# Expert stage: the loop's head on an instruction block, gate/up in two turns on TensorE, a fourth weight buffer, low parts one step later

## The chip, the cores and the metric

One core of a Trainium2 chip runs the whole program. The metric is the device time of one execution in microseconds, the median of the runs. The engines are TensorE (PE), VectorE (DVE), ScalarE (ACT), GpSimd (POOL) and SyncE (SP), which here issues the DMAs of the weights. Each engine has a sequencer of its own that runs that engine's instructions, loops and branches; engines meet at semaphores.

## The reference

One layer of an encoder over 2048 tokens of width 1024. First token mixing: a combined projection, banded attention in 8 heads, differential attention in 4 heads, an output projection. Then channel mixing, in which the change lies: each token goes to 4 of 32 experts.

```
logits = hf @ w_router + b_router;  top_v, top_i = top_k(logits, 4);  top_w = softmax(top_v)
gu   = ragged_dot(xs, w_gate_up, group_sizes) + b_gate_up      # 1024 -> 2 x 1024, per expert
gate = minimum(gu[:, :1024], 7);  up = clip(gu[:, 1024:], -7, 7)
act  = (up + 1) * (gate * sigmoid(1.702 * gate))
y    = ragged_dot(act, w_down, group_sizes) + b_down           # 1024 -> 1024, per expert
out  = segment_sum(y * top_w, token)
```

All of it is in float32.

## The kernel before

Stages 1 and 2 compute the modulation, the normalised input and the attention; stage 3 the output projection, the router and the lists of tokens per expert; stage 4 the experts; stage 5 the final norm. Only stage 4 (`stage4`) is touched. Routing gives every expert its list, and the list is cut into tiles of 320 tokens (`TOK`), the rest going into one tile of 256 (`SMALL`) where it fits. `table` holds the counts. The inputs of this case give 33 tiles, 15 of 320 and 18 of 256.

TensorE, ScalarE and VectorE each run `over_sizes`: a loop over the 32 experts that loads four numbers of the table (the number of large tiles, whether there is a small one, and two from `expert_tiles`), then, under an If, a loop over the large tiles, then, under an If, the small tile. So the code of a tile stands twice in each engine's loop, once for each size. SP and POOL have a loop of their own, `over_tiles`.

A float32 product is made of three products of a shorter format: each operand is split into a high and a low part, and high x high, high x low and low x high are summed in PSUM. A tile's weights are 12 units of 128 x 2048 numbers: 8 units of gate/up (one for each of the 8 blocks of 128 hidden columns, `m`), then 4 of the down projection (`d`). Two units are a pair. SP loads pairs into 3 raw slots (`load_pair`), each when the low parts of the pair that had the slot are made (`lo_ok`). ScalarE makes the high part `hi` (`split_hi`, L1306), VectorE the low part `lo` = raw - hi (`split_lo`, L1347), each into one of `SPL` = 3 buffers. Both are called for the unit `SPL` ahead of the one that TensorE has just used (`split_next`).

Gate/up step `m` on TensorE (L1265 to L1267): 2 outputs x 8 blocks x 3 = 48 matmuls into two of four PSUM banks, after waits for the low part of the unit and, from `m` = 2, for the eviction of step `m` - 2 (`g_ev`). The 8 steps are written out. VectorE evicts gate and up with bias and clamp (L1382, L1386, L1389), makes the low part of the last step's activation (`a_lo`, L1361), then the weights' low part (L1347), waits for ScalarE's sigmoid (L1326), and multiplies (L1394, L1395). ScalarE makes the sigmoid, the weights' high part (L1306), then `a_hi` (L1329).

The down phase has 4 units, 2 column halves x 2 halves of the sum. A step `d` takes the tile's 128-token parts in turn (2 for 256 tokens, 3 for 320, the last of 64), 12 matmuls each (L1287 to L1290). Between them TensorE transposes the next tile's rows in six batches (L1252), which ScalarE and VectorE split into `x_hi` (L1319) and `x_lo` (L1356) from a single PSUM bank. After the odd steps VectorE adds the bias and scales by router weight and gate (`result`, L1369 and L1372). POOL scatters the result rows and adds them in HBM, then gathers the rows of the tile after the next.

Of the kernel before, what the change touches and what calls it, by code (L numbers as in the profile page):

```python
# [1101 lines left out]
def stage4(nc, io, sb, sem, bank, ident, mod_d, acc_d, h2_d, list_d, table):  # L1102
# [9 lines left out]
    RAW, SPL = 3, 3  # L1112
    UPT, PPT = 12, 6
    MT = D // P
    def subtiles(tok):
        return [(s, min(P, tok - s * P)) for s in range(-(-tok // P))]
# [7 lines left out]
    with ExitStack() as ctx:  # L1124
# [30 lines left out]
        LO0 = 2 * RAW  # L1155

# [6 lines left out]
        def over_sizes(eng, tile):  # L1163

            with eng.Fori(0, NE) as e:
                full = eng.value_load(table[0:1, bass.ds(e + 3 * NE, 1)], min_val=0, max_val=CAP // TOK)
                small = eng.value_load(table[0:1, bass.ds(e + 4 * NE, 1)], min_val=0, max_val=1)
                _, before = expert_tiles(eng, e)

                with eng.If(full > 0):  # L1170
                    with eng.Fori(0, full) as r:
                        tile(e, before + r, TOK)
                with eng.If(small > 0):
                    tile(e, before + full, SMALL)
# [31 lines left out]
        with nc.Block() as block:  # L1206
# [37 lines left out]
            def _(pe):  # L1244
# [10 lines left out]
                def tile(e, g, tok):  # L1255
                    pe.wait_ge(xlo_ok, NX * g + NX)
                    for m in range(MT):
                        pe.wait_ge(lo_ok, UPT * g + m + 1 + LO0)
                        if m >= 2:
                            pe.wait_ge(g_ev, 2 * MT * g + 2 * (m - 2) + 2)  # L1260
                        for o in range(2):
                            out = bank[2 * (m % 2) + o][:, 0:tok]
                            for k in range(KT):
                                at = slice((o * KT + k) * P, (o * KT + k + 1) * P)
                                pe.matmul(out, hi[m % SPL][:, at], x_hi[:, k, 0:tok], start=(k == 0), stop=False)  # L1265
                                pe.matmul(out, hi[m % SPL][:, at], x_lo[:, k, 0:tok], start=False, stop=False)  # L1266
                                mm = pe.matmul(out, lo[m % SPL][:, at], x_hi[:, k, 0:tok], start=False,  # L1267
                                               stop=(k == KT - 1))
                            mm.then_inc(gu_mm, 1)
# [32 lines left out]
            def _(act):  # L1302
# [20 lines left out]
                def tile(e, g, tok):  # L1323
                    for m in range(MT):
                        act.wait_ge(g_ev, 2 * MT * g + 2 * m + 1)
                        act.activation(sig[:, 0:tok], gate[:, 0:tok], ACT.Sigmoid, scale=ALPHA).then_inc(sig_ok, 1)  # L1326
                        split_next(m, g)
                        act.wait_ge(a_ok, MT * g + m + 1)
                        act.activation(a_hi[:, m, 0:tok], a[:, m % 2, 0:tok], ACT.Copy).then_inc(ahi_ok, 1)  # L1329
                    for d in range(4):  # L1330
# [12 lines left out]
            def _(dve):  # L1343
# [5 lines left out]
                def split_next(u, g):  # L1349
                    split_lo((u + SPL) % UPT, g + (u + SPL) // UPT)  # L1350
# [24 lines left out]
                def tile(e, g, tok):  # L1375
# [3 lines left out]
                    for m in range(MT):  # L1379
# [8 lines left out]
                        dve.wait_ge(g_ev, 2 * MT * g + 2 * m + 2)  # L1388
                        ch.link(dve.tensor_scalar(up[:, 0:tok], up[:, 0:tok], LIMIT, 1.0, ALU.min, ALU.add))  # L1389
                        if m:  # L1390
                            act_low(g, m - 1, tok)
                        split_next(m, g)
# [3 lines left out]
                        dve.wait_ge(a_ok, MT * g + m + 1)  # L1396
                    act_low(g, MT - 1, tok)
# [4 lines left out]
                    for d in range(4):  # L1402
                        for s, rows in subtiles(tok):
# [4 lines left out]
                        split_next(MT + d, g)  # L1408
                    assert ch.n == NG

                dve.sem_inc(lo_ok, LO0)
                dve.wait_ge(cin, 48)
# [4 lines left out]
                for u in range(SPL):  # L1417
                    split_lo(u, 0)
# [170 lines left out]
```

## Time and profile before

| | |
|---|---|
| median of 3 runs | 5525.59 us (5518.23 to 5529.43) |
| profiled execution, its time and its span | 5522.5 us |
| mean granted TensorE clock | 0.914 |
| TensorE matmul busy | 4660.9 us, 84% of the span |
| TensorE weight loads busy | 3782.0 us, 68% |
| VectorE busy | 3050.0 us, 55% |
| ScalarE busy | 1813.7 us, 33% |
| GpSimd busy | 538.1 us, 10% |
| DMA | 655.59 MB, mean 119 GB/s |

Busy shares are means over stages with different limits; the expert stage is a little over half of the span. A line such as `DVE w_lo L1347` names the engine, the tile written and the line. A "q" behind an engine's name means its sequencer.
### The profile page before, as it was taken

How to read it: one execution, taken by the hardware profiler on the slowest of the kernel's cores; microseconds unless marked ns; L12 is line 12 of the kernel's file. 1: busy time of each engine (PE TensorE's matmuls, PEld its weight loads, DVE VectorE, ACT ScalarE, POOL GpSimd, SP SyncE). 2: the span in 40 equal slices, each digit the busy share in tenths (PEclk: the TensorE clock that was granted, in tenths of full speed). 3: DMA queues.
4: the chain of work that ended last, by engine and by line, in shares of the span. 5: the costliest groups of instructions: out<-in, count | busy, mean ns of one | idle time of the engine just before them, and what ended most of it. 6: DMA issues, size and time to landing. Idle time of an engine off the chain costs nothing. (4 is left out here: it accounts for less than half of the span.)

```text
span 5522.5 us, 75366 instructions
## 1 busy us (share of the span) xinstructions
PE 4660.9 (84%) x25330; PEld 3782.0 (68%) x25331; DVE 3050.0 (55%) x5885; ACT 1813.7 (33%) x2483; POOL 538.1 (10%) x564
## 2 busy tenths in 40 slices
PE   6598987967778658849888999899999999998984
PEld 1565666744545534429787888888888888887873
DVE  3214444065665734436666756666666566666655
ACT  0123333132332312213333433333333333333434
POOL 1000000000000002121111010101010101011111
PEclk9799999988888878869999999999999999999997
DMA  6200001000000042235555555556454456555555
GB/s 228 76 9 20 13 20 32 0 14 11 7 13 3 7 156 76 76 113 174 168 189 173 188 156 183 176 165 191 161 173 165 148 185 199 175 169 184 189 160 204
DMA packets 461031, 655.59 MB, mean 119 GB/s; under 512 B 23036, under 2 KB 334980, under 8 KB 460568
## 3 DMA queue, kind: packets, MB, share of 16 engines
q1 hardware_dynamic: 419240, 523.11, 28.0%
q0 software_dynamic: 39152, 120.42, 8.3%
q10 hardware_dynamic: 2304, 8.39, 0.4%
q8 instruction: 113, 1.85, 0.1%
q14 instruction: 222, 1.82, 0.1%
HBM read 567.71 MB, written 87.27 MB: 119 GB/s over the span
## 5 line engine op out<-in xcount | busy, mean ns | idle before, releaser
L1265 PE MATMUL bank<-x_hi,w_hi 128*128 128x256 f32 (+1 forms) x4224 | 1273.0, 301 | 121.4 <-DVE up L1386 81.2
L1266 PE MATMUL bank<-x_lo,w_hi 128*128 128x256 f32 (+1 forms) x4224 | 1262.8, 299 | 0.0
L1267 PE MATMUL bank<-x_hi,w_lo 128*128 128x256 f32 (+1 forms) x4224 | 1262.0, 299 | 0.0
L1347 DVE TENSOR_TENSOR w_lo<-raw,w_hi 128x2048 fp32r<-128x2048 f32 x399 | 914.6, 2292 | 399.2 <-ACT w_hi L1306 396.5
L1265 PEld LDWEIGHTS bank<-x_hi,w_hi 128*128 128x128 f32 x4224 | 820.5, 194 | 145.2 <-DVE up L1386 90.8
L1306 ACT ACTIVATE w_hi<-raw 128x2048 fp32r<-128x2048 f32 x399 | 759.1, 1903 | 217.5 <-PE bank L1290 167.6
L1266 PEld LDWEIGHTS bank<-x_lo,w_hi 128*128 128x128 f32 x4224 | 821.2, 194 | 0.0
L1267 PEld LDWEIGHTS bank<-x_hi,w_lo 128*128 128x128 f32 x4224 | 819.9, 194 | 0.0
L1287 PE MATMUL bank<-w_hi,a_hi 128*128 128x512 f32 (+1 forms) x1296 | 540.2, 417 | 91.6 <-DVE a_lo L1361 91.6
L1289 PE MATMUL bank<-w_lo,a_hi 128*128 128x512 f32 (+1 forms) x1296 | 519.2, 401 | 0.0
L1290 PE MATMUL bank<-w_hi,a_lo 128*128 128x512 f32 (+1 forms) x1296 | 518.7, 400 | 0.0
L1436 POOL DMA_INDIRECT acc_scratch<-y,idc x102 | 214.8, 2106 | 2193.6 <-DVE y L1372 2172.7
L486 PE MATMUL bank<-v_all,PT 128*128 x2208 | 347.9, 299 | 93.0 <-DVE PT L504 50.5
L486 PEld LDWEIGHTS bank<-v_all,PT 128*128 128x128 f32 x2208 | 291.0, 201 | 152.9 <-issue 82.5
L1329 ACT ACTIVATE a_hi<-a 128x256 fp32r<-128x256 f32 (+1 forms) x264 | 116.8, 442 | 848.6 <-DVE a L1395 848.6
L608 PE MATMUL bank<-k_hi,q 128*128 128x512 f32 (+3 forms) x544 | 227.4, 423 | 171.3 <-DVE k_lo L701 89.9
L1287 PEld LDWEIGHTS bank<-w_hi,a_hi 128*128 128x128 f32 (+1 forms) x1296 | 239.3, 185 | 153.3 <-DVE a_lo L1361 95.9
L724 DVE CUSTOM_DVE_ANT_0 S<-bank,bias 128x512 f32<-128x512 f32 (+3 forms) x544 | 282.6, 559 | 35.4 <-PE bank L608 23.9
L1290 PEld LDWEIGHTS bank<-w_hi,a_lo 128*128 128x128 f32 (+1 forms) x1296 | 237.8, 183 | 70.9
L1289 PEld LDWEIGHTS bank<-w_lo,a_hi 128*128 128x128 f32 (+1 forms) x1296 | 239.7, 185 | 57.1
L646 ACT ACTIVATE S<-S,nm 128x640 f32<-128x640 f32 (+15 forms) x256 | 249.0, 975 | 73.1 <-DVE nm L735 44.3
L893 PE MATMUL bank<-wout,oT 128*128 128x512 f32 x512 | 260.3, 673 | 13.7 <-ACT oT L931 13.7
(211 smaller groups left out, 5695.5 us busy)
## 6 DMA issues: line engine op xcount, KB each, us to landing
raw<-in_w_gate_up SPq DMA_DIRECT2D x268, 1024.0 KB
raw<-in_w_down SPq DMA_DIRECT2D x132, 1024.0 KB
wada<-in_w_ada SPq DMA_DIRECT2D x12, 2048.0 KB, 7.9
bd<-in_b_down SPq DMA_DIRECT2D x33, 512.0 KB
xt<-in_x ACTq DMA_DIRECT2D x16, 512.0 KB, 6.0
o_scratch<-osb SPq DMA_DIRECT2D x128, 64.0 KB, 1.6
ot<-o_scratch SPq DMA_DIRECT2D x16, 512.0 KB, 3.3
xt<-in_x SPq DMA_DIRECT2D x16, 512.0 KB, 3.9
```

Of the source, the lines that this page charges most:

```text
L486: mm = pe.matmul(obank[t % 2][:, h * P:(h + 1) * P], PT[:, i % 4, j * P:(j + 1) * P], v_all[:, kt + j, bass.ds(u * P, P)], start=(first an ...
L646: act.activation(scores(step % 2, c)[:, 0:n], scores(step % 2, c)[:, 0:n], ACT.Exp, bias=nm[:, step % 2, c:c + 1], accum_out=l[:, step % 2 ...
L724: dve.tensor_tensor_reduce(scores(b, c)[:, cs:cs + n * P], sbank[i % 4][:, 0:n * P], add, SCALE, NEG * 8, ALU.add, ALU.max, pm[:, b, c, j: ...
L893: mm = pe.matmul(bank[2 + h][:, :], oT[:, b, k, :], wout[:, k, h * 512:(h + 1) * 512], start=(k == 0), stop=(k == KT - 1))
L1265: pe.matmul(out, hi[m % SPL][:, at], x_hi[:, k, 0:tok], start=(k == 0), stop=False)
L1266: pe.matmul(out, hi[m % SPL][:, at], x_lo[:, k, 0:tok], start=False, stop=False)
L1267: mm = pe.matmul(out, lo[m % SPL][:, at], x_hi[:, k, 0:tok], start=False, stop=(k == KT - 1))
L1287: pe.matmul(out, a_hi[:, k, tk], hi[u % SPL][:, at], start=(kh == 0 and i == 0), stop=False)
L1289: pe.matmul(out, a_hi[:, k, tk], lo[u % SPL][:, at], start=False, stop=False)
L1290: mm = pe.matmul(out, a_lo[:, k, tk], hi[u % SPL][:, at], start=False, stop=(kh == 1 and i == 3))
L1306: act.activation(h, src, ACT.Copy).then_inc(hi_ok, 1)
L1347: dve.tensor_tensor(l, src, h, ALU.subtract).then_inc(lo_ok, 1)
```

## The change

- `SPL` is 4: four buffers each for high and low parts.
- TensorE's gate/up is a loop of two turns of four steps each. The waits for evictions now stand ahead of every step; so that the first two pass, the semaphore `g_ev` starts at `G0` = 4, and all its other users add 4.
- VectorE makes the low part of unit m + 3 (`split_behind`), while ScalarE makes the high part of unit m + 4 in the same step. In gate/up it stands behind the multiplications and ahead of `a_lo`, which is now that of the same step; in the down phase it stands ahead of a step's results, not behind.
- ScalarE makes `a_hi` ahead of the weights' high part.
- `over_sizes` begins with an alignment: the code that follows is placed at the start of an instruction block of 256 on each of the three engines. One of its four table loads is left out, as its number isn't used.

```
--- before.py
+++ after.py
@@ -1109,7 +1109,7 @@
 
 
 
-    RAW, SPL = 3, 3
+    RAW, SPL = 3, 4
     UPT, PPT = 12, 6
     MT = D // P
     def subtiles(tok):
@@ -1153,6 +1153,7 @@
         raw_in = [sem(f"s4_raw_in{i}") for i in range(RAW)]
         NG = 2 * MT
         LO0 = 2 * RAW
+        G0 = 4
 
         def expert_tiles(eng, e):
 
@@ -1162,10 +1163,11 @@
 
         def over_sizes(eng, tile):
 
+            eng.addr_align(256, offset=0, max_nops=0)
             with eng.Fori(0, NE) as e:
                 full = eng.value_load(table[0:1, bass.ds(e + 3 * NE, 1)], min_val=0, max_val=CAP // TOK)
                 small = eng.value_load(table[0:1, bass.ds(e + 4 * NE, 1)], min_val=0, max_val=1)
-                _, before = expert_tiles(eng, e)
+                before = eng.value_load(table[0:1, bass.ds(e + NE, 1)], min_val=0, max_val=TOPK * SEQ // TOK + NE)
 
                 with eng.If(full > 0):
                     with eng.Fori(0, full) as r:
@@ -1253,20 +1255,20 @@
                     mm.then_inc(tx_mm, 1)
 
                 def tile(e, g, tok):
-                    pe.wait_ge(xlo_ok, NX * g + NX)
-                    for m in range(MT):
-                        pe.wait_ge(lo_ok, UPT * g + m + 1 + LO0)
-                        if m >= 2:
-                            pe.wait_ge(g_ev, 2 * MT * g + 2 * (m - 2) + 2)
-                        for o in range(2):
-                            out = bank[2 * (m % 2) + o][:, 0:tok]
-                            for k in range(KT):
-                                at = slice((o * KT + k) * P, (o * KT + k + 1) * P)
-                                pe.matmul(out, hi[m % SPL][:, at], x_hi[:, k, 0:tok], start=(k == 0), stop=False)
-                                pe.matmul(out, hi[m % SPL][:, at], x_lo[:, k, 0:tok], start=False, stop=False)
-                                mm = pe.matmul(out, lo[m % SPL][:, at], x_hi[:, k, 0:tok], start=False,
-                                               stop=(k == KT - 1))
-                            mm.then_inc(gu_mm, 1)
+                    with pe.Fori(0, MT // SPL) as q:
+                        pe.wait_ge(xlo_ok, NX * g + NX)
+                        for j in range(SPL):
+                            pe.wait_ge(lo_ok, UPT * g + SPL * q + j + 1 + LO0)
+                            pe.wait_ge(g_ev, 2 * MT * g + 2 * SPL * q + 2 * j - 2 + G0)
+                            for o in range(2):
+                                out = bank[2 * (j % 2) + o][:, 0:tok]
+                                for k in range(KT):
+                                    at = slice((o * KT + k) * P, (o * KT + k + 1) * P)
+                                    pe.matmul(out, hi[j][:, at], x_hi[:, k, 0:tok], start=(k == 0), stop=False)
+                                    pe.matmul(out, hi[j][:, at], x_lo[:, k, 0:tok], start=False, stop=False)
+                                    mm = pe.matmul(out, lo[j][:, at], x_hi[:, k, 0:tok], start=False,
+                                                   stop=(k == KT - 1))
+                                mm.then_inc(gu_mm, 1)
 
                     pe.wait_ge(xg_in, 16 * NS * g + 32 * NS)
                     for c in range(2):
@@ -1322,11 +1324,11 @@
 
                 def tile(e, g, tok):
                     for m in range(MT):
-                        act.wait_ge(g_ev, 2 * MT * g + 2 * m + 1)
+                        act.wait_ge(g_ev, 2 * MT * g + 2 * m + 1 + G0)
                         act.activation(sig[:, 0:tok], gate[:, 0:tok], ACT.Sigmoid, scale=ALPHA).then_inc(sig_ok, 1)
-                        split_next(m, g)
                         act.wait_ge(a_ok, MT * g + m + 1)
                         act.activation(a_hi[:, m, 0:tok], a[:, m % 2, 0:tok], ACT.Copy).then_inc(ahi_ok, 1)
+                        split_next(m, g)
                     for d in range(4):
                         for s in range(NS):
                             if (d, s) in batch_after[tok]:
@@ -1346,8 +1348,9 @@
                     src, h, l = split_views(u)
                     dve.tensor_tensor(l, src, h, ALU.subtract).then_inc(lo_ok, 1)
 
-                def split_next(u, g):
-                    split_lo((u + SPL) % UPT, g + (u + SPL) // UPT)
+                def split_behind(u, g):
+
+                    split_lo((u + SPL - 1) % UPT, g + (u + SPL - 1) // UPT)
 
                 def x_low(g, j):
                     (s, rows), h = subs[j // 2], j % 2
@@ -1385,36 +1388,36 @@
                         dve.wait_ge(gu_mm, 2 * MT * g + 2 * m + 2)
                         dve.tensor_scalar(up[:, 0:tok], bank[2 * (m % 2) + 1][:, 0:tok], bcur[:, MT + m:MT + m + 1], -LIMIT,
                                           ALU.add, ALU.max).then_inc(g_ev, 1)
-                        dve.wait_ge(g_ev, 2 * MT * g + 2 * m + 2)
+                        dve.wait_ge(g_ev, 2 * MT * g + 2 * m + 2 + G0)
                         ch.link(dve.tensor_scalar(up[:, 0:tok], up[:, 0:tok], LIMIT, 1.0, ALU.min, ALU.add))
-                        if m:
-                            act_low(g, m - 1, tok)
-                        split_next(m, g)
                         dve.wait_ge(sig_ok, MT * g + m + 1)
                         ch.link(dve.tensor_tensor(gate[:, 0:tok], gate[:, 0:tok], sig[:, 0:tok], ALU.mult))
                         dve.tensor_tensor(a[:, m % 2, 0:tok], up[:, 0:tok], gate[:, 0:tok], ALU.mult).then_inc(a_ok, 1)
-                        dve.wait_ge(a_ok, MT * g + m + 1)
-                    act_low(g, MT - 1, tok)
+                        if m < MT - 1:
+                            split_behind(m, g)
+                        act_low(g, m, tok)
+                    split_behind(MT - 1, g)
 
                     dve.wait_ge(bd_in, 16 * g + 16)
                     dve.wait_ge(idc_ok, NS * g + NS)
                     dve.wait_ge(sc, 16 * NS * g + 16 * NS)
                     for d in range(4):
+                        split_behind(MT + d, g)
                         for s, rows in subtiles(tok):
                             if d % 2 == 1:
                                 result(g, d // 2, s, rows, tok)
                             if (d, s) in batch_after[tok]:
                                 x_low(g + 1, batch_after[tok][d, s])
-                        split_next(MT + d, g)
                     assert ch.n == NG
 
                 dve.sem_inc(lo_ok, LO0)
+                dve.sem_inc(g_ev, G0)
                 dve.wait_ge(cin, 48)
 
                 dve.memset(xg[:, :, :], 0.0).then_inc(cleared, 1)
                 dve.wait_ge(cleared, 1)
                 dve.memset(y[:, :, :], 0.0).then_inc(go, 1)
-                for u in range(SPL):
+                for u in range(SPL - 1):
                     split_lo(u, 0)
                 for j in range(NX):
                     x_low(0, j)
```

## Rows read from the trace of the kernel before

**Rows 1.** Windows: start:end, length, busy us per engine (instructions), granted clock, DMA share, GB/s.

```profile
3008.20:3094.60 86.40, 75.29 (x504) 69.64 (x504) 55.50 (x77) 32.68 (x36) 11.70 (x12) 0.92 0.58 182
...
3094.60:3187.00 92.40, 92.19 (x552) 83.22 (x552) 61.10 (x80) 33.59 (x35) 11.48 (x12) 1.00 0.57 178
...
4576.50:4653.00 76.50, 71.25 (x505) 66.22 (x504) 58.39 (x78) 34.98 (x37) 16.55 (x13) 1.00 0.67 214
...
2491.20:5451.80 2960.60, 2751.16 (x17352) 2509.63 (x17352) 1917.20 (x2535) 1097.64 (x1154) 398.19 (x382) 0.96 0.55 174
```

**Rows 2.** Waits of 2480 to 5452 us: who, for whom, total us, times, longest.

```profile
DVE w_lo L1347 <- ACT w_hi L1306: 393.4, 393, 1.6
...
DVE bcur L1377 <- issue: 346.8, 32, 14.4
...
PE bank L1287 <- DVE a_lo L1361: 91.6, 18, 6.0
...
PE bank L1265 <- DVE up L1386: 81.2, 22, 7.9
...
ACT L1326 <- issue: 43.0, 32, 3.0
```

**Rows 3.** Timeline of VectorE and TensorE at a turn: start, us, instruction, idle before.

```profile
3024.32 0.17 DVE L1377 COPY bcur<-bgu 128x16 f32 x1 [12.11 <-issue]
...
3025.56 0.58 PE L1265 MATMUL bank<-x_hi,w_hi 128*128 128x256 f32 x1 [5.46 <-DVE up L1386]
```

**Rows 4.** Sequencer instructions of single lines: ns min/median/max, first and last start.

```profile
L1165 PEldq COMPARE_BRANCH  x32: 79/214/3548, 2564.9 to 5445.5; - x32
...
L1165 DVEq COMPARE_BRANCH  x1: 63/63/63, 3010.0 to 3010.0; - x1
L1165 DVEq FUSED_REGOPS  x1: 74/74/74, 3015.7 to 3015.7; - x1
...
L1170 DVEq COMPARE_BRANCH  x1: 56/56/56, 3020.5 to 3020.5; - x1
...
L687 DVEq FUSED_REGOPS  x1: 63/63/63, 490.4 to 490.4; - x1
```

**Rows 5.** Readers of `tile_table`: the load at the loop's head that the change leaves out.

```profile
L1159 DVEq TENSOR_LOAD <-tile_table x32: 298/432/991, 2487.4 to 5373.7; - x32
```

**Rows 6.** DMA queue of instructions, 3008 to 3026 us: packets, MB, share of the engines.

```profile
q14 instruction: 4, 0.03, 0.5%
```

**Rows 7.** Timeline of VectorE in gate/up: two low parts one step apart.

```profile
3039.37 2.29 DVE L1347 TENSOR_TENSOR w_lo<-raw,w_hi 128x2048 fp32r<-128x2048 f32 x1 [1.11 <-ACT w_hi L1306]
...
3045.36 2.29 DVE L1347 TENSOR_TENSOR w_lo<-raw,w_hi 128x2048 fp32r<-128x2048 f32 x1 [1.11 <-ACT w_hi L1306]
```

**Rows 8.** Timeline of TensorE in the small tile that starts at 4576.51.

```profile
4622.58 0.40 PE L1287 MATMUL bank<-w_hi,a_hi 128*128 128x512 f32 x1
...
4628.06 0.60 PE L1252 MATMUL bank<-ident,xg 128*128 128x128 f32 x4
4630.53 0.50 PE L1287 MATMUL bank<-w_hi,a_hi 128*128 128x512 f32 x1 [1.88 <-DVE a_lo L1361]
...
4653.01 0.38 PE L1265 MATMUL bank<-x_hi,w_hi 128*128 128x256 f32 x1 [3.37 <-issue]
```

**Rows 9.** Groups by line, 3008 to 3094 us; then the DMA queue, 3066 to 3073.

```profile
L1347 DVE TENSOR_TENSOR w_lo<-raw,w_hi 128x2048 fp32r<-128x2048 f32 x12 | 27.5, 2293 | 12.5 <-ACT w_hi L1306 12.5
...
L1306 ACT ACTIVATE w_hi<-raw 128x2048 fp32r<-128x2048 f32 x12 | 22.8, 1900 | 2.4 <-PE bank L1290 2.4
...
L1356 DVE TENSOR_TENSOR x_lo<-bank,x_hi 128x512 fp32r<-128x512 f32 (+1 forms) x6 | 3.6, 598 | 1.5 <-ACT x_hi L1319 1.5
...
L1372 DVE SCALAR_TENSOR_TENSOR y<-y,idc,gtf 128x512 f32<-128x512 f32 x4 | 3.0, 753 | 0.3
...
L1369 DVE TENSOR_TENSOR y<-bank,bd 128x512 f32<-128x512 f32 x4 | 2.8, 688 | 2.1 <-PE bank L1290 2.1
...
q1 hardware_dynamic: 2049, 2.07, 88.8%
```

## The prediction

> **What bounds the kernel now.** I read the windows first. The expert stage is 2960.6 us of the span [rows 1] and consists of 33 tiles, 18 of 256 tokens and 15 of 320. The reader is to compare three tiles there: a 320-token tile takes 92.4 us with TensorE busy 92.21, a 256-token tile in the middle takes 86.4 us with TensorE busy 75.29 at a granted clock of 0.92, and one 256-token tile, the second of its expert, takes 76.5 us at a clock of 1.00. So the large tiles are bound by TensorE, and the small ones lose some 10 to 20 us each.
>
> The waits say to what [rows 2]. TensorE waits 91.6 us, 18 times, ahead of the down projection for `a_lo`, 81.2 us ahead of a gate/up step for the eviction `up`. VectorE itself waits 346.8 us, 32 times, ahead of the first instruction of a tile (`bcur`) for nothing visible, and 393.4 us for ScalarE's `w_hi`. These two are the roots; POOL's and ScalarE's waits end ahead of nothing that TensorE waits for.
>
> Root one is the turn of the expert loop on VectorE. In [rows 3] `bcur` starts after 12.11 us idle. Its sequencer shows where they go [rows 4]: the branch back is taken at 3010.0 and the head goes on at 3015.7, 5.5 us later; the head (four table loads) lasts to 3020.5; the branch over the large body is taken there, and `bcur` behind it starts at 3024.3, 3.6 us of fetch later. The same turn costs ScalarE 43.0 us in 32 times, 1.3 us each, head and all [rows 2]. Instruction packets land in just these gaps: four of 8 KB between 3008 and 3026 [rows 6]. So the program's own code is being fetched. TensorE has it too, seldom: its branch back takes 79 ns to 3548 ns, median 214 [rows 4]; eight turns are slow (3.3 to 3.6), each at the end of a small tile that followed a large one.
>
> Root two is VectorE's step. Two `w_lo` in a row start 5.99 us apart, and 1.11 us of it is the wait for the `w_hi` that ScalarE makes in the same step [rows 7]. TensorE needs 384 matmuls x 0.120 us / 8 = 5.76 us a step of 256 tokens: 4576.51 to 4622.58 for eight [rows 8]. VectorE is thus slower than TensorE by 0.23 a step, never recovers what the turn cost, and hands the debt to TensorE twice: 5.46 us ahead of step 2 and again ahead of the second down step. [rows 3, 8] show one of each. A wait of over 2 us is followed by a granted clock of one half (1.2 of 2.4 GHz) for 3.4 or 6.8 us; hence the 0.92 of the middle tile in [rows 1]. With 320 tokens TensorE's step is 56.3/8 = 7.04 us, which covers 5.98.
>
> **The change part by part.**
> Low parts one step later. VectorE's `w_lo` in step m takes unit m+3, whose `w_hi` ScalarE made a step before, so the 1.11 us wait goes: 5.99 - 1.11 = 4.88 us of work a step (the same instructions in another order). ScalarE now does sigmoid, `a_hi`, then `w_hi` (1.90 us, [rows 9]); `a_hi` is done some 0.5 us after `a`, beside the 2.29 us of `w_lo`, so `a_lo` behind it doesn't wait. What is late next is TensorE: 5.76 against 4.88, a reserve of 0.88 us a step that repays debts.
>
> Four buffers. Unit m+3's low part goes into the buffer of unit m-1, which TensorE has left. The price is that ScalarE wants the raw weights a step earlier, relative to the release of their slot (by the low part). A pair is loaded after the low part of unit 2P-5 and read at the high part of 2P, four steps less the 4.5 us within a step, some 18 to 20 us. The load of 2.07 MB took 7 us [rows 9], 10 beside gathers. Covered; the cost without that cover is a rival below.
>
> Down phase. VectorE makes the low part first, then results and `x_lo`; for the odd steps that is 2.29 + 2 x (0.69 + 0.75) + 0.69 [rows 9] = 5.9 us in a step of TensorE of 2 x 12 x 0.231 + 0.7 = 6.2. I lay the order out: the high part of unit 0 of the next tile can start only when the first down step is complete (5.9), is ready at 8.4, its low part at 10.7, then a result to 12.1 and `x_lo` to 12.8, which the third transpose wanted at 11.8: 1.0 us of TensorE waiting. At the end of the tile the last `x_lo` is 0.9 us late instead of 0.4. Bounds: nothing (if these hide), and one `w_lo` in each of two places, 2 x 2.29 = 4.6 us. I take 1.5 us a small tile, near the laid out order, and 0 for a large one (8.3 us a step).
>
> The wait at the down phase. With VectorE in step, `a_lo` of the last unit is done 2.8 us after gate/up ends, and TensorE wants it at 5.9. The 1.9 to 6.0 us go.
>
> The turn. One table load (`L1159`) goes on three engines: median 0.43 us on VectorE [rows 5], plus about 0.3 around it; on TensorE 0.3. With fetches gone, VectorE's gap is 3.7 to 4 us of head from about 0.6 us after the tile's last `x_lo`; it reaches `bcur` 5 us after TensorE has begun, and the first eviction is wanted at 2.9 and 5.8: no wait at step 2. Fetching itself: TensorE's loop holds 552 + 504 pairs of load and matmul [rows 1], some 2200 instructions with waits; rolling takes 192 pairs off each body, leaving about 1430. Attention loops of 1530 and 1650 instructions turn with no fetch at all, and between 488 and 942 us no packet of their queue, `q8`, stands. So TensorE's slow turns go: 8 x 3.4 = 27 us, in part inside the tiles counted below. The inner turn costs the sequencer a branch of 0.2 us and a few register instructions; the sequencer runs about 3.4 us ahead of the array in the down phase and about 1.8 in gate/up, which hides 0.2 to 0.6. Bounds: 0 and one slow branch, 3.5 us.
> VectorE's loop has about 300 instructions before and 290 after. In the trace ScalarE loops of 185 and 201 don't fetch when they turn, a VectorE loop of 472 does (branch at 487.5, next instruction at 490.4, [rows 4]), and that of 300 does. The order of the packets fits blocks of 8 KB of which four are held, one of them fetched ahead: from its present place the loop touches four and the one ahead throws out the head; from a block's start it touches three. Then all four stay and both fetches go. That is my choice; the cost if it is wrong is small, see the first rival.
>
> **Sum.** A small tile: gate/up 46.07, first down step 5.83 (4622.58 to 4628.41), the rest 19.1 (4630.53 to 4653.01 less its gap of 3.37), head 0.4, plus 1.5: 72.9; the head is 0.4 shorter at best, so 72.5. A large one: 92.4 as in [rows 1]. 18 x 72.5 + 15 x 92.4 = 2691, against 2960.6: 270 us less. The profiled execution's time and span are both 5522.5; 5522.5 - 270 = 5252.5, and the median of the runs stands 3.1 above: 5256, which I call 5255.
>
> **Rivals.**
> A, VectorE's branch back still fetches, only the inner one is cured. For: 290 instructions lie between those that stay and those that don't, and nothing shows four blocks rather than three. Then `bcur` comes 5.5 us later, the first evictions end at 11.6 us where TensorE wants them at 11.5, and 0.88 a step repays it by step 6. About 1 us a small tile: 5255 + 18 = 5273.
> The Trainium skill (Runtime: NRT & Kernel Launch, Instruction fetch mechanics) says that such an engine holds two blocks of 16 KiB, 256 instructions each, and that a taken branch out of them must fetch. The stall agrees with the trace; the block size does not, since the packets are 8 KB. By the page, 290 instructions from a block's start fill two blocks, the one fetched ahead replaces the first, and A is what happens.
> B, the alignment cures nothing and both fetches stay, 9 us. Then evictions come at 15 us against 11.5: 3.6 us of wait, and half clock behind it for 3.4 or 6.8 us, 1.7 to 3.4 us lost: some 6 us for 18 small tiles, 108 us: 5363. Against: 300 is well under 472.
> C, TensorE's inner branch fetches at each tile. 3.4 us plus 1.7 to 3.4 for the clock, 33 tiles: 168 to 224 us, 5423 to 5479. Against: loops four times as long hold.
> D, slower: the supply of raw weights. Two MB must land within about 18 us. If loads took 28 us beside gather and scatter, each of six pairs a tile would hold up ScalarE, and then all, for some 10 us: 33 x 60 - 270, far over. The point from which it decides is 8.2 us a tile (270/33), 1.4 us a pair, loads of 20 us. For: a small tile asks its 12.6 MB of weights in 72 us rather than 86. Against: the engines' share is 0.67 in the tile of 76.5 us [rows 1], and loads of 7 to 10.
>
> **How the numbers follow.** Forecast 0.68, A 0.15, B 0.08, C 0.06, D 0.03. The likeliest's own range is small tiles of 71 to 75.5 and large of 92.0 to 93.2: 2658 to 2757, so 5223 to 5322. A lies within it. With a little for the half of B: 5215 to 5335; C, D and most of B are left out, 0.17. Within 0.2% (what a measurement can tell) is 5515 to 5537; no case aims there, 0.01. Faster 0.96, slower 0.03.
>
> **What would show it.** Right: `bcur`'s idle near 4 us with no 8 KB packets in the expert stage; `w_lo` not waiting for `w_hi` in gate/up; TensorE's waits for `up` and for `a_lo` each under 10 us in all; granted clock 0.99 or more in the stage; small tiles of 71 to 74. A: an idle of about 9 with the other signs intact. B: 12 and `up` waits again. C: a gap of 3 us in the middle of gate/up. D: ScalarE's `w_hi` waiting for a DMA of `raw`. Wrong in size: transposes or the first gate/up matmul waiting for `x_lo` more than 2 us a tile. Small tiles over 80 us would refute the mechanism.

## The result, and the profile after

The changed kernel takes 5261.84 us, the median of 4 runs (5260.7 to 5265.46); the kernel before, run beside it, 5521.91 (5516.68 to 5529.43). The ratio is 0.9536, 95% interval 0.9521 to 0.9552: 260 us less. Forecast were 5255 in a range of 5215 to 5335.

The page of the changed kernel: busy time by engine; of the 40 slices TensorE's row and its granted clock; and the instruction queues.

```profile
span 5259.2 us, 75068 instructions
...
PE 4573.7 (87%) x25330; PEld 3717.5 (71%) x25331; DVE 3020.5 (57%) x5885; ACT 1818.2 (35%) x2484; POOL 487.1 (9%) x564
...
PE   6598888977687767883999999999999999999994
...
PEclk9799999989888887886999999999999999999997
...
q8 instruction: 33, 0.54, 0.0%
q14 instruction: 67, 0.55, 0.0%
```

In the 20th to the 39th slice, the expert stage, TensorE is at nine tenths or more. TensorE ran as many matmuls as before (25330) with 87 us less busy time, 85 of them in the stage, where the granted clock rose from 0.96 to 1.00: a matmul at half clock is busy for longer.

Windows of a 256-token tile, a 320-token tile and the stage, with the columns of [rows 1].

```profile
2806.70:2879.40 72.70, 71.23 (x504) 66.24 (x504) 54.47 (x76) 32.88 (x36) 10.05 (x12) 1.00 0.70 216
3024.90:3117.00 92.10, 92.08 (x553) 83.24 (x553) 60.02 (x79) 33.30 (x35) 11.85 (x12) 1.00 0.54 171
2494.20:5188.10 2693.90, 2666.50 (x17352) 2443.56 (x17352) 1888.89 (x2534) 1099.16 (x1154) 348.35 (x381) 1.00 0.60 190
```

The stage went from 2960.6 to 2693.9 us, 266.7 less, and that is the whole gain (263.3 between the two profiled spans, as the stage also begins 3.0 us later): the large tile kept its time, the small one went from 86.4 (the middle one of [rows 1]) to 72.7, at full clock.

The waits of 2480 to 5250 us on VectorE and TensorE (answering [rows 2]):

```profile
DVE up L1389 <- PE bank L1269: 394.8, 264, 3.0
...
DVE w_lo L1349 <- ACT w_hi L1308: 100.4, 99, 1.4
DVE bcur L1380 <- issue: 77.9, 32, 3.4
...
PE bank L1254 <- DVE x_lo L1359: 17.1, 20, 1.4
PE bank L1267 <- DVE x_lo L1359: 11.2, 17, 0.7
PE bank L1267 <- issue: 10.8, 1, 10.8
```

The roles are exchanged: VectorE now waits in each of the 264 steps for TensorE, 1.5 us on average, and TensorE's waits for `up` and `a_lo` are gone. In the stage TensorE waits 39 us in all, 28 of them for `x_lo`. VectorE at a turn and in gate/up, to be laid beside [rows 3] and [rows 7]:

```profile
2806.99 0.75 DVE L1375 SCALAR_TENSOR_TENSOR y<-y,idc,gtf 128x512 f32<-128x512 f32 x1
2810.04 0.17 DVE L1380 COPY bcur<-bgu 128x16 f32 x1 [2.31 <-issue]
...
2831.73 2.29 DVE L1349 TENSOR_TENSOR w_lo<-raw,w_hi 128x2048 fp32r<-128x2048 f32 x1
...
2835.76 0.49 DVE L1389 TENSOR_SCALAR up<-bank,bcur 128x256 f32<-128x256 f32 x1 [1.01 <-PE bank L1269]
...
2837.50 2.28 DVE L1349 TENSOR_TENSOR w_lo<-raw,w_hi 128x2048 fp32r<-128x2048 f32 x1
```

The turn costs 2.31 us instead of 12.11. Two low parts start 5.77 us apart, TensorE's own pace, and 1.01 of it is VectorE waiting: its step holds 4.76 us of work.

The branch back on the three sequencers (answering [rows 4]; ns), then the instruction queues from 2500 to 5150 us:

```profile
L1167 PEldq COMPARE_BRANCH  x32: 76/209/216, 2564.7 to 5183.3; - x32
...
L1167 DVEq COMPARE_BRANCH  x32: 50/63/74, 2569.4 to 5188.1; - x32
```

```profile
q8 instruction: 2, 0.03, 0.0%
q14 instruction: 3, 0.02, 0.0%
```

No turn of TensorE is slow any more (longest 216 ns; 3548 before). In the same stretch of before the two rows read:

```profile
q8 instruction: 73, 1.20, 0.2%
q14 instruction: 140, 1.15, 0.1%
```

A row with 0.1% of the DMA engines thus stood behind most of the 347 us that VectorE waited at its turns (78 are left without it): it is the instant of such packets that counts, not their share.

### The profile page after: what moved, and what is told of

It is laid out like the page before. It is cut to its first block and busy times, and to the rows that moved or that the text cites. A ratio compares the mean times of both kernels' runs of the same rounds, so it can differ in the third digit from the quotient of the medians.

```text
span 5259.2 us, 75068 instructions
## 1 busy us (share of the span) xinstructions
PE 4573.7 (87%) x25330; PEld 3717.5 (71%) x25331; DVE 3020.5 (57%) x5885; ACT 1818.2 (35%) x2484; POOL 487.1 (9%) x564
## 5 line engine op out<-in xcount | busy, mean ns | idle before, releaser
L1267 PE MATMUL bank<-x_hi,w_hi 128*128 128x256 f32 (+1 forms) x4224 | 1249.4, 296 | 22.3 <-DVE x_lo L1359 11.2
L1269 PE MATMUL bank<-x_hi,w_lo 128*128 128x256 f32 (+1 forms) x4224 | 1246.1, 295 | 0.0
L1268 PE MATMUL bank<-x_lo,w_hi 128*128 128x256 f32 (+1 forms) x4224 | 1246.1, 295 | 0.0
L1267 PEld LDWEIGHTS bank<-x_hi,w_hi 128*128 128x128 f32 x4224 | 803.5, 190 | 35.6 <-issue 35.5
L1268 PEld LDWEIGHTS bank<-x_lo,w_hi 128*128 128x128 f32 x4224 | 803.5, 190 | 0.0
L1269 PEld LDWEIGHTS bank<-x_hi,w_lo 128*128 128x128 f32 x4224 | 803.5, 190 | 0.0
L1289 PE MATMUL bank<-w_hi,a_hi 128*128 128x512 f32 (+1 forms) x1296 | 525.2, 405 | 0.0
L1389 DVE TENSOR_SCALAR up<-bank,bcur 128x256 f32<-128x256 f32 (+1 forms) x264 | 135.9, 515 | 394.8 <-PE bank L1269 394.8
L1439 POOL DMA_INDIRECT acc_scratch<-y,idc x102 | 157.9, 1548 | 1940.2 <-DVE y L1375 1919.3
L506 ACT ACTIVATE PT<-bank 128x384 f32<-128x384 f32 (+2 forms) x192 | 98.1, 511 | 508.4 <-PE bank L474 508.3
```

Source lines behind the costliest of these rows:

```text
L1267: pe.matmul(out, hi[j][:, at], x_hi[:, k, 0:tok], start=(k == 0), stop=False)
L1268: pe.matmul(out, hi[j][:, at], x_lo[:, k, 0:tok], start=False, stop=False)
L1269: mm = pe.matmul(out, lo[j][:, at], x_hi[:, k, 0:tok], start=False, stop=(k == KT - 1))
L1289: pe.matmul(out, a_hi[:, k, tk], hi[u % SPL][:, at], start=(kh == 0 and i == 0), stop=False)
```

## The experiments

Each was timed in 3 rounds against the kernel before, whose medians lay between 5520.7 and 5523.3.

**The alignment alone,** on the kernel before.

```
 def over_sizes(eng, tile):
+    eng.addr_align(256, offset=0, max_nops=0)
     with eng.Fori(0, NE) as e:
```

> The kernel before with the loop's head on an instruction block and nothing else. Theory (VectorE's code fetch at the turn starts the debt, its 5.99 us step keeps it): the fetches go on VectorE, its idle ahead of bcur falls from 12 to about 4 us, the 5.5 us wait ahead of step 2 goes; the step is still 0.23 us longer than TensorE's, so about 2 us of wait for a_lo remain per small tile and TensorE's own slow turns (its loop still has 2200 instructions) stay. Small tiles about 77 us, large 92.4 to 93: about 5350 us. Rival 1 (the order of low parts is what matters): within 30 us of the kernel before. Rival 2 (alignment is all): within 20 us of the changed kernel, 5262.

5332.98 us, ratio 0.9662 (0.9646 to 0.9678): 188 us of the 260 with one line, and 17 more than was expected. The waits of its stage, then its instruction queues:

```profile
DVE w_lo L1348 <- ACT w_hi L1307: 347.1, 394, 1.6
...
DVE bcur L1378 <- issue: 52.5, 32, 4.1
...
PE bank L1288 <- DVE a_lo L1362: 41.3, 18, 2.8
PE bank L1266 <- issue: 38.6, 17, 7.7
```

```profile
q8 instruction: 80, 1.31, 0.2%
q14 instruction: 2, 0.02, 0.0%
```

VectorE's loop of 299 instructions, four blocks touched from its old place, needs three from a block's start; its queue `q14` falls silent. What is left is what the other edits answer to: the wait for `w_hi`, the debt at `a_lo`, and TensorE's fetches. VectorE's four table loads at the loop's head are the same instructions as before; one of them, before and here (ns, min/median/max):

```profile
L1167 DVEq TENSOR_LOAD <-tile_table x32: 301/1006/1116, 2486.7 to 5372.2; - x32
```

```profile
L1168 DVEq TENSOR_LOAD <-tile_table x32: 302/310/323, 2484.6 to 5182.8; - x32
```

The medians of the four add up to 2.83 us before and to 1.22 here: where code is fetched at the turn, the loads beside it are slow too.

**The change without the alignment.**

```
-            eng.addr_align(256, offset=0, max_nops=0)
```

> The changed kernel without the alignment. Theory of four held blocks of 8 KB: VectorE's loop has 283 instructions instead of 299, and from the place that the packets of the trace before suggest (about 96 instructions into a block of 128) it ends at about 380 of 384, so it touches three blocks and does not fetch: within 5 us of the changed kernel. If my place is off by a few instructions it touches four, both fetches stay, and the reserve of 0.88 us a step must pay for 9 us: small tiles about 78 us, total about 5360. Rival (alignment is unneeded because the new order covers every fetch): fetches seen in the trace, time still 5262.

5262.73, ratio 0.9534 (0.9518 to 0.955): the alignment is worth nothing here. VectorE's loop is now 283 instructions, and from slot 96 to 98 of its block (an estimate from the order of the packets of before) it ends at 379 to 381, just ahead of 384: three blocks by luck. The stage begins 3.7 us earlier (2490.5, not 2494.2), and its first three tiles give that back and some 2.6 us more; a TensorE branch of 3.4 us at 2654.0, with 3.2 us of waiting behind it, is part of that.

**VectorE's loop head at slot 128, and at slot 108.**

```
+            if eng.engine == mybir.EngineType.DVE:
+                eng.addr_align(256, offset=127, max_nops=0)    # head at 128; offset=107: head at 108
+            else:
                 eng.addr_align(256, offset=0, max_nops=0)
```

> The changed kernel with VectorE's loop head 128 instructions behind the start of a 256 block (the other engines as changed). Theory (blocks of 128 instructions, four held, one fetched ahead): 128 + 283 = 411 touches three blocks, no fetch at a turn, 5262 within 5 us. Rival (blocks of 256, two held): the loop lies in two such blocks as before and behaves as in the changed kernel too, but then the next run can't differ from this one.

> The changed kernel with VectorE's loop head 108 instructions behind the start of a block, 20 ahead of the run before. Theory: 108 + 283 = 391 touches a fourth block of 128 and the block ahead of it throws out the head: both fetches come back on VectorE (5.5 and 3.5 us). bcur then comes about 12 us after TensorE's first gate/up matmul, its first evictions end at 13.3 where 11.5 is wanted: 1.8 us of wait and perhaps half clock behind it, 2 to 3.5 us for each small tile: 5295 to 5325. Rival 1 (the reserve of the new order pays for all of it): fetches in the trace and 5262. Rival 2 (as my prediction priced both fetches): 5363. Rival 3 (place does not matter): no fetches, 5262.

The head at 128: 5262.96, ratio 0.9531 (0.9516 to 0.9547), no fetch. The head at 108, where 283 instructions reach into a fourth block: 5328.69, ratio 0.9654 (0.9638 to 0.967), 66 us more for the same instructions 20 slots ahead. The upper end of what was expected was passed by 4. Waits and queues of the latter:

```profile
DVE bcur L1383 <- issue: 319.7, 32, 14.0
...
PE bank L1270 <- DVE up L1392: 46.5, 19, 5.0
```

```profile
q14 instruction: 151, 1.24, 0.2%
```

This is the forecast's rule shown from both sides: counted in blocks of 128 instructions (a packet of 8 KB), a loop that touches three turns freely, and one that touches four fetches at its head and at an If. Blocks of 256 don't explain it, as the loop lies in two of them from either place. That one of the blocks held is fetched ahead shows at this kernel's first turn (branch back at 2568.59, next instruction at 2571.37). The queue from 2567 to 2568.5 us, then VectorE:

```profile
q14 instruction: 1, 0.01, 2.1%
```

```profile
2567.71 0.68 DVE L1375 TENSOR_TENSOR y<-bank,bd 128x512 f32<-128x512 f32 x1
2568.49 0.75 DVE L1378 SCALAR_TENSOR_TENSOR y<-y,idc,gtf 128x512 f32<-128x512 f32 x1
2575.19 0.17 DVE L1383 COPY bcur<-bgu 128x16 f32 x1 [5.94 <-issue]
```

The packet, at 2567.90 for 0.51 us, comes as the loop enters its fourth block, and no instruction waits for it; the next one, at 2569.60, is what the branch waits for. The reading that fits is that of the forecast: four blocks held, and one that nobody needs yet has taken the place of the head. It is also rival B's state, and B was priced too high: 108 us by the forecast, 66 here. `bcur` comes 7.6 us later a turn (319.7 against 77.9 in 32), but TensorE waits only 2.4 us for `up` on average in 19 tiles (4.0 to 5.0 in the seven small ones behind a large one, 1.2 to 2.2 in the nine others, 0.3 to 0.5 in three large ones), and half clock follows for 37.5 us.

**TensorE's gate/up written out again.**

```
-                    with pe.Fori(0, MT // SPL) as q:
-                        pe.wait_ge(xlo_ok, NX * g + NX)
-                        for j in range(SPL):
+                    pe.wait_ge(xlo_ok, NX * g + NX)
+                    for m in range(MT):
...
```

> The changed kernel with TensorE's gate/up steps written out again (2200 instructions in its loop), all else as changed. Theory: TensorE's eight slow branches of 3.4 us at the ends of small tiles that follow a large one come back; the half clock behind them costs 1.7 us more: 8 x 3.4 to 8 x 5.1, 27 to 41 us above the changed kernel, about 5295. Rival: the rolling is worth nothing (within 10 us), or costs, because the inner branch is on the path (faster than the changed kernel).

5305.29, ratio 0.9609 (0.9593 to 0.9625): 43 us more, and 2 over the upper end of what was expected. Eight turns are slow again, but each for 5.2 us of TensorE's idle time, not 3.4; the branch itself takes up to 6066 ns. Why was the next question.

**The same with three buffers.**

```
-    RAW, SPL = 3, 4
+    RAW, SPL = 3, 3
```

> The kernel with TensorE's steps written out (5305 us in its run) with three buffers instead of four, low parts still made one step after the high parts, so VectorE's step m makes unit m+2. Theory (the fourth buffer gives slack that nobody uses): the low part of m+2 is ready about 4.5 us after TensorE ends step m, which wants it after 5.76 us; in the down phase it is earlier still: 5305 within 5 us. Rival (the later low part needs the fourth buffer): TensorE waits for w_lo in gate/up, at least 0.5 us in each of 8 steps of 18 small tiles, 5377 or more.

5276.73, ratio 0.956 (0.9544 to 0.9576): the expected time was missed by 28 us, on the good side. The fourth buffer isn't what removes the wait for `w_hi`: with three that row is 101.7 us as with four, all of it in the down phase, and a small tile without a slow turn takes 72.5. But the slow branches were 3.3 to 3.9 us against 5.9 to 6.1. In the records of the packets the first of each slow turn starts 0.94 to 1.04 us after the branch here, and 3.5 to 3.7 after it with four buffers: with four, the low parts and hence the loads of weights come a step earlier, and one of them is under way when the branch wants its code. The fourth buffer has one other use, which this run leaves out with the rolled loop: a turn of `SPL` steps in which each step has its fixed buffer divides the 8 steps of gate/up when `SPL` is 4, not when it is 3.

**Four buffers, loads a step later,** to test that.

```
-                    sp.wait_ge(lo_ok, UPT * g + 2 * p + 2)
+                    sp.wait_ge(lo_ok, UPT * g + 2 * p + 3)
```

> The kernel with gate/up written out on TensorE and four buffers (5305.29), with one edit: each pair of weights is loaded when one more low part has been made, a step of TensorE later. In that kernel a slow turn of TensorE (branch 5.87 to 6.07 us) had its code packet start 3.5 to 3.7 us after the branch, at the end of a 2 MB load of weights; with three buffers, where the low parts and with them the loads come a step later, the packet started 0.95 us after the branch and the branch took 3.3 to 3.9. Theory (the packet waits behind the load of weights): here the branches take 3.3 to 3.9 us, TensorE's idle ahead of L1267 in the 8 slow turns falls from 49 to about 29 us, half clock from 48 to under 25, and the time is 5275 to 5283. Rival (it is the number of buffers, or the place of the code): branches stay at 6 and the time at 5305. Second rival (the later load itself costs): weights arrive late, ScalarE's w_hi waits for a DMA, over 5305.

5278.58, ratio 0.9557 (0.9541 to 0.9573), the three-buffer kernel's time within what can be measured. DMA traffic around the same slow turn, busy tenths in 40 slices of a window of 15 us, and TensorE's first matmul behind the turn; first the kernel with the earlier loads, from 3276 us (branch at 3280.7, taking 6.06):

```profile
DMA  0000049499999999999999200000001000094969
```

```profile
3289.58 0.63 PE L1267 MATMUL bank<-x_hi,w_hi 128*128 128x320 f32 x1 [5.18 <-issue]
```

Then this kernel, from 3270 us (branch at 3274.8, taking 3.68):

```profile
DMA  9930000000000002000000284999999999999999
```

```profile
3281.35 0.48 PE L1267 MATMUL bank<-x_hi,w_hi 128*128 128x320 f32 x1 [2.81 <-issue]
```

In the first the engines are full of weights from 3278 to 3284.3, and the code packet starts at 3284.41; in the second they are empty, and it starts at 3275.81. A code fetch that meets a load of 2 MB waits for its end: so it is in all eight slow turns of the kernel with the earlier loads, and in none of this one, where the packet starts 0.97 to 1.51 us after the branch. TensorE's waits for "issue" went from 49.4 to 29.9 us; without the stage's first, which is no turn, from 41.8 to 23.5 in the eight turns. Half clock around the first seven of them went from 48 to 27 us, where under 25 was expected. The other rivals, the number of buffers and a late load, are out.

**The old order of VectorE and ScalarE,** with the rest of the change: `a_lo` of the step before and the low part of unit m + 4 ahead of the sigmoid wait, low parts last in a down step, ScalarE's high part ahead of `a_hi`.

```
                         dve.wait_ge(sig_ok, MT * g + m + 1)
...
-                        if m < MT - 1:
-                            split_behind(m, g)
-                        act_low(g, m, tok)
+                        dve.wait_ge(a_ok, MT * g + m + 1)
```

> The changed kernel with the old order on ScalarE and VectorE (low part of the unit whose high part is made in the same step, and ahead of the multiplications; in the down phase behind the results), with four buffers, the alignment and TensorE's rolled loop kept. Theory: VectorE's step is 5.99 us again against 5.76, so TensorE waits 2 to 3 us for a_lo in each small tile; the waits for x_lo in the down phase (0.8 + 0.4 us) go in exchange. The aligned-only kernel's 5333 less the 43 us of TensorE's own fetches: 5290, small tiles of 74. Rival (four buffers alone uncouple the two): w_lo's wait for w_hi gone and 5240.

5308.79, ratio 0.9612 (0.9595 to 0.9628): with no code fetched at all, the order is worth 47 us, 19 more than expected.

```profile
DVE w_lo L1349 <- ACT w_hi L1308: 341.0, 396, 1.4
...
PE bank L1289 <- DVE a_lo L1363: 36.8, 18, 2.3
```

Small tiles take 73.9 to 76. The 18 waits at the down phase, 2.0 us each, and the half clock that follows them (37.5 us of it) are the price; in exchange TensorE waits 15 us for `x_lo` instead of 28.

**`x_lo` ahead of the result** in the down phase.

```
                         for s, rows in subtiles(tok):
-                            if d % 2 == 1:
-                                result(g, d // 2, s, rows, tok)
                             if (d, s) in batch_after[tok]:
                                 x_low(g + 1, batch_after[tok][d, s])
+                            if d % 2 == 1:
+                                result(g, d // 2, s, rows, tok)
```

> The changed kernel with x_lo made ahead of a result where both stand behind the same part of a down step. Theory: the changed kernel's remaining waits, 0.82 us ahead of the third transpose and 0.66 us (of which 0.2 to 0.4 is the loop's head on TensorE) ahead of the first gate/up matmul, come from x_lo standing behind the result's 1.44 us. Both go: 1.0 to 1.3 us a small tile, 18 to 24 us in all, about 5241. Rival (the results are now late for TensorE's third down step instead): same time within 5 us, with a wait for y in the place of that for x_lo.

5231.75 (5229.1 to 5234.86), ratio 0.9478 (0.9462 to 0.9494): faster than both kernels, 30 us under the changed one and 9 better than expected. A small tile, and the waits for `x_lo`:

```profile
2878.00:2949.00 71.00, 71.00 (x507) 66.47 (x506) 54.61 (x76) 32.91 (x35) 13.87 (x13) 1.00 0.69 222
```

```profile
PE bank L1267 <- issue: 10.7, 1, 10.7
PE bank L1254 <- DVE x_lo L1359: 2.3, 2, 1.4
```

TensorE is busy for the whole 71.0 us: this tile is bound by it. It is 1.7 us shorter, of which the two waits for `x_lo` of the changed kernel's small tile, 0.82 ahead of the third transpose and 0.66 ahead of the next tile, make 1.5.

**Loads two and three low parts later,** for the slower rival, on the changed kernel.

```
-                    sp.wait_ge(lo_ok, UPT * g + 2 * p + 2)
+                    sp.wait_ge(lo_ok, UPT * g + 2 * p + 4)      # the other: + 5
```

> The changed kernel (5261.84) with each pair of weights loaded two low parts later, so that from the start of a load to the high part that reads it there are some 10 us of TensorE's steps (two of 5.76 less 1.5) and not 21.5. It measures how much room the supply of weights has, the slower rival of the prediction. Theory (a load takes 7 to 8 us, and the prepared units hide what comes late): no change, 5258 to 5268. Rival (two MB beside gather and scatter take longer than 10 us often, and ScalarE's lateness reaches TensorE): waits of w_hi for raw that end in waits of TensorE for w_lo, 5290 or more.

> The same with three low parts later: 4.3 us from the start of a load to where its high part stood before, so each comes 3 to 4 us late, and the load of a pair now waits for the low part of the pair just ahead of it: load 7.5, high part 1.9, low part 2.3, together 11.7 us a pair, against 11.52 of TensorE in a small tile's gate/up and 14.1 in a large one. Theory (this ring then sets the pace in small tiles and with gathers beside it costs some us each, large tiles stay at 92): 18 x 2 to 18 x 10 us more, 5300 to 5440, with TensorE waiting for w_lo and VectorE for w_hi, ScalarE for raw. Rival (the supply is not near any limit): under 5275.

Two later: 5261.32, ratio 0.9527 (0.9511 to 0.9543), the changed kernel's time; ScalarE waits for weights 16 times, 2.2 us at most, and TensorE's waits stay as they were. Three later: 5576.16, ratio 1.0102 (1.0085 to 1.0119), 1% over the kernel before and 136 us over the upper end of what was expected. ScalarE in the latter's small tile (start, us, instruction, idle before):

```profile
2910.50 1.90 ACT L1308 ACTIVATE w_hi<-raw 128x2048 fp32r<-128x2048 f32 x1
2912.30 0.57 ACT L1321 ACTIVATE x_hi<-bank 128x512 fp32r<-128x512 f32 x1
2921.10 1.91 ACT L1308 ACTIVATE w_hi<-raw 128x2048 fp32r<-128x2048 f32 x1 [8.23 <-DMA raw<-in_w_gate_up]
2922.92 0.58 ACT L1321 ACTIVATE x_hi<-bank 128x512 fp32r<-128x512 f32 x1
```

The expectation counted the ring of weights alone. But ScalarE works in order: while it waits 8.23 us for weights, the split of the next transposed rows stands behind it, and TensorE, which has one bank for transposes, waits 6 to 8 us for `x_lo` in every small tile and 1 to 3 in most large ones (193 us in 67 waits); behind that it waits 45 us for `a_lo`, and half clock stands for 212 us. Small tiles take 86.6 and large ones, which were expected to stay, 96.2: (86.6 - 72.8) x 18 + (96.2 - 92.1) x 15 = 310 of the 314.

## Why the prediction was right

**The bound and the two roots.** They held. The alignment alone, which changes no instruction of a tile, took VectorE's idle time ahead of `bcur` from 347 to 52 us and the time down by 188; the order alone is worth 47 once no code is fetched. The two overlap: with the new order the fetches cost only 66 (the head at 108), since 5.77 - 4.76 = 1.0 us of reserve a step repays most of the debt, as the forecast had it.

**Low parts one step later.** Forecast was 4.88 us of VectorE's work a step; 4.76 measured. The wait for `w_hi` vanished in gate/up, with 99 left in the down phase. `a_hi` before `w_hi` cost nothing: `a_lo` waits 16.8 us in 33 times.

**Four buffers.** "Covered" was right with room: in a small tile's gate/up the load starts 19.5 to 21.6 us ahead of its reader (18 to 20 forecast), and 8 to 10 us, in the run with loads two low parts later, change nothing. That the buffer was needed to free `w_lo` is not so, as three do the same without it (with TensorE's steps written out; the loop in turns of four steps needs four). Its own effect is to move the loads a step ahead, which alone costs nothing and beside a code fetch costs 2.4 us a turn.

**Down phase.** Forecast: 1.0 us ahead of the third transpose and 0.5 more at the tile's end, 1.5 in all; measured 0.82 and 0.66, of which the kernel before had 0.4 already, as in its tile of 3008 us:

```profile
3008.34 0.38 PE L1265 MATMUL bank<-x_hi,w_hi 128*128 128x256 f32 x1 [0.41 <-DVE x_lo L1356]
```

The place and the mechanism were right, and reversing two lines there takes 1.7 us off each small tile. I priced this wait, but left it standing as the price of the order; it was the order's one avoidable part.

**The wait at the down phase** is gone: there is no row for `a_lo` on TensorE.

**The turn.** No fetch at a turn on any engine, as forecast. The size of VectorE's gap was off: 2.3 us where 3.7 to 4 stood. That sum took the head as the kernel before ran it, and there the table loads were slow beside the fetches (medians of 0.43 to 1.01 us, [rows 5] shows the fastest of the four); the three that are left take 0.30 each. With slack behind `bcur` this moved nothing. TensorE's eight slow turns went; that saving was put at 27 us, and undoing it cost 43 with the loads where they are and 17 with the loads elsewhere (5278.58 - 5261.84). The rolled loop's inner branch cost nothing that the tiles show.

**The sum.** Small tiles 72.8 against 72.5, large ones 92.1 against 92.4: these cancel. The stage took 2693.9 against 2691, and it begins 3.0 us later (2494.2, not 2491.2), with 10.8 us of TensorE's idle time ahead of its first matmul (6.17 before). The sum has no term for that; with it, and the measured 266.7 in place of 270, 5522.5 - 266.7 + 3.0 = 5258.8 against a span of 5259.2. The late start needs both the alignment and TensorE's rolled loop: without the alignment the stage begins at 2490.5, with the steps written out at 2492.0. Behind the head's branch on TensorE (2485.4) two packets of `q8` stand ahead of the changed kernel's first matmul at 2494.2 (2486.3 and 2490.9, the second taking 1.4 us); before, the matmul at 2491.2 came between the two (2488.4 and 2492.4), and so it does in every run that lacks one of the two edits. That points to a wait for the second packet; it was not tested, and why that place of the code needs it stays open.

**The rivals.** A (the branch back still fetches) is refuted for this place. The Trainium skill (Runtime: NRT & Kernel Launch, Instruction fetch mechanics) gives such an engine 32 KiB in blocks of 16 KiB; the packets here are 8 KB, and a loop of 283 instructions that begins at a block's start turns with none, where two blocks with one fetched ahead would miss. The four blocks of 8 KB that these runs show do make the page's 32 KiB; its 2048 instructions for TensorE agree with the loop of about 2200 that fetches and the one of 1419 that doesn't. B exists, in the kernel with the head at 108, at 66 us of its 108. C (the inner branch of TensorE fetches) left no trace. D (supply) begins between two and three low parts later: the forecast put the point of decision at loads of 20 us against loads of 7 to 10, and by the runs a start 8 to 10 us ahead still suffices, while with a third low part, by which a load also waits for the pair just ahead of it, it doesn't.

## What to carry to other kernels

Where an engine sits idle at a loop's turn for "issue", look at the instruction queues in that instant, count the loop's instructions and see how many blocks it touches from where it stands; shortening it, moving its head, or rolling an inner part can be worth more than any instruction in it. A cure by luck of place (the change without its alignment) can be lost by the next edit, as the head at slot 108 costs 66 us here, so the alignment is worth keeping though it measures nothing. Then give the engine that keeps step with TensorE some reserve in each step, and within a step put what TensorE waits for (`x_lo`) ahead of what only a store waits for.

## What the runs showed of the hardware

- VectorE's code comes in packets of 8 KB, TensorE's in packets of 16 KB. On VectorE, 283 instructions in three blocks go on 0.24 to 0.28 us behind the branch back; in four blocks it takes 2.7 to 5.8 us, and again 2.3 to 5.8 at an If.
- A code packet waits for a load of weights that is under way: about 1.0 us from TensorE's branch to the packet (0.94 to 1.04 in the kernel with three buffers), 3.5 to 3.7 behind 2 MB. The branch takes 3.3 to 3.9 us in the one case and 5.9 to 6.1 in the other. So the time of a load can cost an engine that doesn't use it.
- Register loads of VectorE's sequencer are slow beside code fetches: the four of the loop's head had medians that add up to 2.83 us with fetches at the turn and to 1.22 without.
- The granted clock was 1.00 through the whole stage once TensorE's waits, but for the stage's first, were under 1.5 us each. With 18 waits of about 2.0 us (the old order) it stood at half for 37.5 us, and around seven waits of 5.2 us (TensorE's steps written out) for 48.
